# Input projection of a decoder layer: RMS factor applied to the products in place of the input, weights second in the load queue, squares added on VectorE

## The reference, cut to what matters

```python
def rms_norm(x, g):
    xf = x.astype(jnp.float32)
    xf = xf * lax.rsqrt(jnp.mean(xf * xf, axis=-1, keepdims=True) + EPS)
    return xf.astype(x.dtype) * g

def layer_front(x, norm1_g, w_in, q_norm_g, k_norm_g):
    xn = rms_norm(x, norm1_g)
    proj = xn @ w_in
    q, k, v, a, gt = jnp.split(proj, ...)
    q = rms_norm(q.reshape(hs), q_norm_g)     # per head of 64
    k = rms_norm(k.reshape(hs), k_norm_g)
    v = v.reshape(hs)
    u = a * jax.nn.sigmoid(gt)
    return q, k, v, u
```

## Time and profile before

| | us |
|---|---|
| three runs | 1910.13, 1910.41, 1918.43 |
| median | 1910.41 |
| the profiled execution | 1909.07 |
| its span, first to last instruction | 1907.4 |
| TensorE busy in the span | 1809.6 (95%) |
| DVE busy | 1482.6 (78%) |
| POOL busy | 1065.8 (56%) |
| ACT busy | 824.4 (43%) |

### The profile page before, as it was taken

How to read it: one execution, slowest core, us unless ns; L and a number is a source line. 1 busy time by engine, 2 the same in 40 slices (tenths; PEclk the granted TensorE clock), 3 DMA queues, 4 the chain that set the end, 5 groups by cost and what they waited for, 6 DMA issues and landing times.

```text
span 1907.4 us, 38904 instructions
## 1 busy us (share of the span) xinstructions
PE 1809.6 (95%) x14571; PEld 1717.1 (90%) x14571; DVE 1482.6 (78%) x2730; ACT 824.4 (43%) x1101; POOL 1065.8 (56%) x813
## 2 busy tenths in 40 slices
PE   6988988989899999999999999999999999999996
PEld 6988765449899999999999999999999999999995
DVE  3659675541588988985776699999999999999973
ACT  4233665432322445555776444444444444434421
POOL 3232222222224888875564777777777777777720
PEclk8999999989899999999999999999999999999997
DMA  4362877872122677766676999999999999999961
GB/s 158 94 118 99 280 260 271 301 267 97 67 89 96 210 230 229 221 221 207 231 279 263 323 348 349 365 351 360 348 373 354 358 350 375 351 357 358 344 221 69
DMA packets 207319, 488.43 MB, mean 256 GB/s; under 512 B 34161, under 2 KB 119218, under 8 KB 187090
## 3 DMA queue, kind: packets, MB, share of 16 engines
q1 hardware_dynamic: 145474, 315.97, 48.2%
q0 software_dynamic: 55296, 167.94, 23.7%
q10 hardware_dynamic: 6416, 2.78, 1.2%
HBM read 445.95 MB, written 40.66 MB: 255 GB/s over the span
## 4 chain that ended last, share of the span: by engine, by line
PE 84%; DVE 7%; ACT 4%; issue 1%; POOL 1%; DVEq 1%; DMA 1%; ACTq 0%; POOLq 0%
PE pair L1554 24%; PE pair L1556 24%; PE pair L1555 24%; PE pair L1886 3%; DVE conv L1088 3%; PE pair L1699 2%; PE pair L1711 1%; PE pair L1837 1%; PE pair L1751 1%; PE pair L1564 1%; PE pair L1664 1%; PE pair L1686 1%; POOL w_lo L645 1%; ACT page_kt L820 1%; ACT w_hi L968 1%
## 5 line engine op out<-in xcount | busy, mean ns | idle before, releaser
L1554 PE MATMUL pair<-x_hi,w_hi 128*128 128x256 f32 (+2 forms) x2064 | 604.0, 293 | 17.7 <-DVE x_lo L1044 13.7
L1555 PE MATMUL pair<-x_lo,w_hi 128*128 128x256 f32 (+2 forms) x2064 | 596.0, 289 | 0.0
L1556 PE MATMUL pair<-x_hi,w_lo 128*128 128x256 f32 (+2 forms) x2064 | 594.8, 288 | 0.0
L1554 PEld LDWEIGHTS pair<-x_hi,w_hi 128*128 128x128 f32 x2064 | 393.2, 190 | 20.6 <-issue 14.9
L1555 PEld LDWEIGHTS pair<-x_lo,w_hi 128*128 128x128 f32 x2064 | 392.9, 190 | 0.2
L1556 PEld LDWEIGHTS pair<-x_hi,w_lo 128*128 128x128 f32 x2064 | 391.4, 190 | 0.0
L657 POOL DMA_INDIRECT v_rows<-in_v_t,at_row x256 | 302.8, 1183 | 135.2 <-DVE pair L1443 81.7
L1443 DVE SCALAR_TENSOR_TENSOR pair<-v_rows,share,pair 128x1024 f32<-128x1024 f32 x254 | 327.4, 1289 | 23.6 <-issue 0.9
L650 POOL DMA_INDIRECT picked_a<-acts_sparse,at_unit x256 | 284.1, 1110 | 92.4 <-issue 77.7
L1554 PE MATMUL pair<-a_hi,w_hi 128*128 128x288 f32 x1024 | 308.2, 301 | 17.8 <-DVE w_lo L1505 17.8
L1556 PE MATMUL pair<-a_hi,w_lo 128*128 128x288 f32 x1024 | 307.3, 300 | 0.0
(11 more groups left out here) (223 smaller groups left out, 3326.6 us busy)
## 6 DMA issues: line engine op xcount, KB each, us to landing
w_raw<-in_u_t SPq DMA_DIRECT2D x72, 1024.0 KB, 5.2
v_raw<-in_u_t SPq DMA_DIRECT2D x53, 1024.0 KB
w_raw<-in_v_t SPq DMA_DIRECT2D x128, 256.0 KB
v_raw<-in_v_t SPq DMA_DIRECT2D x128, 256.0 KB, 4.4
gates<-g_out SPq DMA_DIRECT2D x9, 2048.0 KB, 8.2
g_in<-gates SPq DMA_DIRECT2D x16, 1152.0 KB
v_ring<-in_cache_v SPq DMA_DIRECT2D x64, 256.0 KB, 3.8
v_ring<-in_cache_v POOLq DMA_DIRECT2D x64, 256.0 KB, 4.4
```

Source lines behind the costliest of these rows:

```text
L1554: te.matmul(out, s_hi, m_hi, start=start, stop=False)
L1555: te.matmul(out, s_hi, m_lo, start=False, stop=False)
L1556: return te.matmul(out, s_lo, m_hi, start=False, stop=stop)
```

## The change

The gain `g1` alone is multiplied into `x` before the split; the token's factor is left out of the projection's input and applied to what comes out of it:

- gates: DVE multiplies the PSUM result by `rstd` into `sq` (`scale_gate`), ACT takes the sigmoid in place, DVE multiplies the sigmoid by `rstd` once more, so that `u = a * (sigmoid * rstd)`;
- q and k: TensorE transposes `rstd` so that the factor stands along the partitions (`turn_rho`, kept by DVE in `rho`); ACT's square takes it as its scale, and DVE's scaling becomes a product with two factors;
- v: ACT's copy takes it as its scale.

The sum of squares: ACT squares the 8 blocks of `x` into the 4 blocks of `q_t` and the 4 of `k_t` (free at that time), DVE adds them in three steps, and TensorE sums over the features once (`sum_first`, a pair of matmuls) inside chunk 1, into `pair[3]`. The order of loads becomes `g1`, `x` part 0, weights 0, `x` parts 1 to 3, weights 1. The low part of chunk 0 moves from POOL to DVE, in two halves. POOL sets `eps` first, and ACT takes a square of it before anything else. Two of the first seven taps move behind the scaling of the second pair of gates.

```diff
+            sp.dma_start(g1[:, :], io["norm1_g"]).then_inc(gain_loaded, 16)
             for part in range(4):
                 two_blocks = slice(2 * part, 2 * part + 2)
                 sp.dma_start(resid[:, two_blocks, :], io["x_t"][:, two_blocks, :]).then_inc(x_loaded[part], 16)
-            load_weights(0)
+                if part == 0:
+                    load_weights(0)
             load_weights(1)
-            sp.dma_start(g1[:, :], io["norm1_g"]).then_inc(small_loaded, 16)
...
-            for chunk in range(N_IN + 1):
+            pool.wait_ge(w_split, 1)
+            for chunk in range(1, N_IN + 1):
...
-            sc.wait_ge(const_ready, 1)
-            squares(sq, resid, KD, lambda kd: sc.wait_ge(x_loaded[kd // 2], 16), sum1_done, sq1_done,
-                    lambda kd: high_w(0) if kd == KD - 3 else None)
-            root(pair[0], D, sum1_done, KD, root1_done)
-            high_x(scaled1, high1)
-            high_w(1)
+            sc.wait_ge(eps_ready, 1)
+            sc.activation(rstd[:, 0:1], eps[:, :], ACT.Square)
+            for kd in range(KD):
+                sc.wait_ge(scaled1, kd + 1)
+                sc.activation(x_hi[:, kd, :], conv[:, kd % 4, :], ACT.Copy).then_inc(high1, 1)
+                if kd == 1:
+                    high_w(0)
+                elif kd == KD - 3:
+                    high_w(1)
+                sc.activation(squared(kd), resid[:, kd, :], ACT.Square).then_inc(sq1_done, 1)
+            high_w(2)
+            root(pair[3], D, sum1_done, 1, root1_done)
...
                 for cb in range(2):
-                    sc.wait_ge(projected, 2 * chunk + cb + 1)
-                    if n:
-                        sc.wait_ge(u_done, cb + 1)
-                    sc.activation(two(sq[:, cb, :]), halves(pair[cb]), ACT.Sigmoid).then_inc(gate_sig, 1)
-                high_w(chunk + 2)
+                    sc.wait_ge(gate_scaled, 2 * n + cb + 1)
+                    sc.activation(sq[:, cb, :], sq[:, cb, :], ACT.Sigmoid).then_inc(gate_sig, 1)
+                if n:
+                    high_w(chunk + 2)
...
+            def scale_x(kd):
+                v.wait_ge(x_loaded[kd // 2], 16)
+                v.tensor_scalar(conv[:, kd % 4, :], resid[:, kd, :], g1[:, kd:kd + 1], None, ALU.mult).then_inc(scaled1, 1)
+            def low_x(kd):
+                v.wait_ge(high1, kd + 1)
+                v.tensor_tensor(x_lo[:, kd, :], conv[:, kd % 4, :], x_hi[:, kd, :].bitcast(F32), ALU.subtract)\
+                    .then_inc(x_ready, 1)
+            def low_first_w():
+                v.wait_ge(w_high, 1)
+                for first in (0, WC // 2):
+                    mine = slice(first, first + WC // 2)
+                    last = v.tensor_tensor(w_lo[:, 0, mine], w_raw[:, 0, mine], w_hi[:, 0, mine].bitcast(F32), ALU.subtract)
+                last.then_inc(w_split, 1)
+            v.wait_ge(gain_loaded, 16)
+            scale_x(0)
+            for kd in range(1, KD):
+                scale_x(kd)
+                low_x(kd - 1)
+                if kd == 2:
+                    low_first_w()
+            low_x(KD - 1)
+            v.wait_ge(sq1_done, KD)
+            v.tensor_tensor(q_t[:, :, :], q_t[:, :, :], k_t[:, :, :], ALU.add)
+            v.tensor_tensor(q_t[:, 0:2, :], q_t[:, 0:2, :], q_t[:, 2:4, :], ALU.add)
+            v.tensor_tensor(q_t[:, 0, :], q_t[:, 0, :], q_t[:, 1, :], ALU.add).then_inc(squares_added, 1)
...
-            normed(g1, root1_done, scaled1, high1, x_ready)
+            reciprocal_rms(root1_done)
+            def scale_gate(n):
+                for cb in range(2):
+                    v.wait_ge(projected, after_projection(2 * n) - 1 + cb)
+                    v.tensor_tensor(two(sq[:, cb, :]), halves(pair[cb]), two(rstd[:, :]), ALU.mult).then_inc(gate_scaled, 1)
...
             for n in range(2):
+                scale_gate(n)
+                if n:
+                    taps_of(0, 2)
+                for cb in range(2):
+                    v.wait_ge(gate_sig, 2 * n + cb + 1)
+                    v.tensor_tensor(sq[:, cb, :], sq[:, cb, :], rstd[:, :], ALU.mult)
...
                 if n == 0:
-                    taps_of(0, FIRST_TAPS)
+                    taps_of(0, FIRST_TAPS - 2)
+            v.wait_ge(rho_turned, 1)
+            v.tensor_copy(rho[:, 0:NT - 1], pair[1][:, 1, 0:P].rearrange("p (t x) -> p t x", x=32)[:, :, 0])
+            v.tensor_copy(rho[0:NDEC, NT - 1:NT], pair[1][0:NDEC, 1, P:P + 1]).then_inc(rho_kept, 1)
...
-                    v.tensor_tensor(dst.rearrange("p (h d) -> p h d", d=HD),
-                                    pair[m % 4 // 2][0:r, m % 2, 0:WCOL].rearrange("p (h d) -> p h d", d=HD),
-                                    ss.unsqueeze(2).to_broadcast([r, 4, HD]), ALU.mult).then_inc(qk_scaled, 1)
+                    v.scalar_tensor_tensor(dst.rearrange("p (h d) -> p h d", d=HD),
+                                           pair[m % 4 // 2][0:r, m % 2, 0:WCOL].rearrange("p (h d) -> p h d", d=HD),
+                                           rho[0:r, nt:nt + 1], ss.unsqueeze(2).to_broadcast([r, 4, HD]),
+                                           ALU.mult, ALU.mult).then_inc(qk_scaled, 1)
...
-            te.wait_ge(const_ready, 1)
-            sum_squares(pair[0], sq, KD, sq1_done, sum1_done)
+            def sum_first():
+                te.wait_ge(squares_added, 1)
+                te.wait_ge(const_ready, 1)
+                for half in range(2):
+                    last = te.matmul(pair[3][:, half, 0:HALF], ones[:, :], q_t[:, 0, HALF * half:HALF * (half + 1)],
+                                     start=True, stop=True)
+                last.then_inc(sum1_done, 1)
+            def turn_rho():
+                for nt in range(NT):
+                    r = ROWS[nt]
+                    last = te.transpose(pair[1][0:r, 1, 32 * nt:32 * nt + 32], rstd[0:32, P * nt:P * nt + r], ident[0:32, 0:32])
+                last.then_inc(rho_turned, 1)
...
-                    te.wait_ge(root1_done, 1)
                     chunk_product(0, x_ready)
...
-                    if chunk == 2:
-                        te.wait_ge(gate_sig, cb + 1)
+                    if chunk == 1 and cb == 1:
+                        te.wait_ge(root1_done, 1)
+                    elif chunk == 2:
+                        te.wait_ge(gate_scaled, cb + 1)
...
-                    block_product(banks, chunk % 2, cb).then_inc(projected, 1)
+                    between = (lambda n: sum_first() if n == 1 else None) if chunk == 1 and cb == 0 else None
+                    block_product(banks, chunk % 2, cb, between).then_inc(projected, 1)
...
                     if m == 0:
-                        te.wait_ge(gate_sig, 4)
+                        te.wait_ge(gate_scaled, 4)
+                        turn_rho()
+                    elif m == 3:
+                        te.wait_ge(rho_kept, 1)
```

More of the change, by code:

```diff
@@ L382, in build_layer, with squared @@
     up_done, gelu_done, a_done, down_done, added = sem("up_done"), sem("gelu_done"), sem("a_done"), sem("down_done"), sem("added")
-    SMALL_LOADS = 7
+    eps_ready, gain_loaded, squares_added = sem("eps_ready"), sem("gain_loaded"), sem("squares_added")
+    gate_scaled, rho_turned, rho_kept = sem("gate_scaled"), sem("rho_turned"), sem("rho_kept")
+    rho = stats[:, 80:80 + NT]
+    def squared(kd):
+        return (q_t if kd < PAIRS else k_t)[:, kd % PAIRS, :]
+    SMALL_LOADS = 6
     STORES = 4 + 2 + 1 + CC
@@ L597, in _ @@
         def _(pool):
+            pool.memset(eps[:, :], EPS).then_inc(eps_ready, 1)
             pool.memset(ones[:, :], 1.0)
@@ L601, in _ @@
             pool.memset(own[:, :, :], 0.0)
-            pool.memset(eps[:, :], EPS)
             pool.memset(u_p[:, :, 0:PAD], 0.0)
@@ L760, in _ @@
                             sc.wait_ge(u_done, 4)
-                        sc.activation(sq[0:r, m % 2, 0:WCOL], src, ACT.Square).then_inc(qk_sq, 1)
+                        sc.wait_ge(rho_kept, 1)
+                        sc.activation(sq[0:r, m % 2, 0:WCOL], src, ACT.Square, scale=rho[0:r, nt:nt + 1]).then_inc(qk_sq, 1)
                         sc.wait_ge(qk_sum, m + 1)
@@ L766, in _ @@
                     else:
-                        sc.activation(v_nat[0:r, nt, WCOL * (chunk - 4):WCOL * (chunk - 3)], src, ACT.Copy)\
+                        sc.activation(v_nat[0:r, nt, WCOL * (chunk - 4):WCOL * (chunk - 3)], src, ACT.Copy, scale=rho[0:r, nt:nt + 1])\
                             .then_inc(v_kept, 1)
@@ L1054, in normed @@
                 low(KD - 1)
+            def scale_x(kd):
[5 more added lines that the diff above has]
+                    .then_inc(x_ready, 1)
+                if kd % 2:
+                    v.drain()
+            def low_first_w():
[14 more added lines that the diff above has]
+            v.tensor_tensor(q_t[:, :, :], q_t[:, :, :], k_t[:, :, :], ALU.add)
+            v.drain()
+            v.tensor_tensor(q_t[:, 0:2, :], q_t[:, 0:2, :], q_t[:, 2:4, :], ALU.add)
+            v.drain()
```

(2 more changed lines are left out.)

## The result

The kernel after the change takes 1957.91 us (median; 1953.46 to 1962.09), the kernel before beside it 1910.78 (1910.13 to 1918.43). The ratio is 1.0235, interval 1.0211 to 1.0259: **2.4% slower**, 47 us, where 1899.9 was forecast. The profiled execution of after took 1953.46, its span is 1951.8.

What follows compares the result with a forecast made beforehand. TensorE was taken as the bound (84% of the chain), behind a front delay of 24.58 us. Terms -11.8 - 0.2 - 0.6 + 1.05 + 0.75 + 0.3 = -10.5 took 1910.41 to 1899.9 us, range 1897.5 to 1904.5.

Steps and rivals of the forecast that it cites:

- Start: Front of the kernel: TensorE's first product comes at 12.75 us in place of 24.58, worth -11.8 us.
- Clock: TensorE's first products: low clock for 2.9 to 5.9 us (13 to 26 products), taken as -0.6 us.
- Summing pair: TensorE's queue in chunk 1: one added pair of matmuls summing the squares, +1.05 us.
- Transposes: TensorE's queue: five added transposes of rstd, about +0.75 us, range 0.4 to 1.2.
- The covers: Projection chunks: new waits for squares, root, reciprocal, gates and chunk 4's weights hidden by slack, the last 1.6 to 2.3 us.
- Rival A: Chunk 4's weights: thin cover gives way, TensorE 2.5 to 3 us late, total 1903; chance 0.20.
- rival B: DVE is the bound: its added 5.1 us find no idle time, gain 5.4, total 1905; chance 0.10.
- The collision: Chunk 1: low_x(6) on DVE waits for POOL's low part until 22.7 us, costing TensorE 0 to 0.3 us.
- Products with two factors: DVE's 20 tiles: 0.782 against 0.721 us each, +0 to +1.2 us, taken +0.3.
- the whole shifts: Everything after the front (attention, output projection, mixer) moves earlier by the front's whole gain, -10.5 us.
- Rival D: TensorE's clock stays low beyond chunk 0; 1916.5 us if chunks 0 and 1 are all low; chance 0.03.
- C: Start doesn't matter, a later stage being set by something that doesn't move (pages, stores); about 1909 us; chance 0.05.

Runs made afterwards that it cites:

- e1: Changed kernel with 46 instructions of fulfilled waits ahead of TensorE's first product; 1980.1 against 1995.82 us for the kernel before, ratio 0.9935.
- e5: Changed kernel with 46 instructions of waiting ahead of TensorE's work, timed in more rounds; 1982.29 against 1997.2 us for the kernel before, ratio 0.9927.
- e6: Changed kernel with 46 waiting instructions, low part of weights 0 back on POOL in one piece; 1987.9 us, ratio 0.9954 to the kernel before.
- e7: Changed kernel with 46 waiting instructions, weights 0 loaded behind all four parts of x again; 1982.36 us, ratio 0.9949 to the kernel before.
- e8: Kernel before with only weights 0 issued between the first and second part of x; 1996.34 us, ratio 1.0005 to the kernel before.
- e10: Changed kernel with 37 instructions of waiting ahead of TensorE's work; 1977.2 us in one run, kernel before beside it 1983.18.
- e11: Changed kernel with 225 instructions of waiting ahead of TensorE's work; 2010.41 us in one run.
- e4: Changed kernel with 24 instructions of fulfilled waits ahead of TensorE's first product; 2046.75 us, ratio 1.0287 to the kernel before.
- e9: Changed kernel with 33 instructions of waiting ahead of TensorE's work; 2061.2 us in one run, kernel before beside it 1983.18.
- e2: Kernel before with 210 instructions of fulfilled waits in TensorE's queue behind the sums of the squares; 2039.99 us, ratio 1.0258 to the kernel before.
- e12: Changed kernel with 250 instructions of waiting ahead of TensorE's work; 2038.64 us in one run.

## Why the prediction was wrong, point by point

- **Start** (-11.8): measured 12.69 against the worked-out 12.75, **-11.9**. Right, with each term of its queue: scale 2 at 9.05, the low part of weights 0 at 10.28, two halves in 2.36.
- **Clock** (-0.6): low for 3.9 us, inside the 2.9 to 5.9 that were given; 17 products in place of 26, -0.9.
- **Summing pair** (+1.05): 29.61 to 30.33, **+0.72**, cheaper than half of the row of eight passes (2.10): in that row, at the granted clock 1.00, the first pass after 1.16 us of idleness holds up the second for 0.34, and the last counts with its whole 0.39, while in after passes start 0.23 apart and the next product 0.03 behind the last one. **Transposes** (+0.75): 63.91 to 64.30, about **+0.4**.
- **The covers.** No wait at the pair, at `pair[3]`, at the gates or at chunk 4; TensorE waits for nothing from 12.69 to 64.30. But the slack of chunk 4 was thinner than said. POOL's low part ended at 63.35 and was wanted at 64.30: 0.95 us, not 1.6 to 2.3. Rival A came near.
- **DVE** (rival B): its 17 us of waiting were used up wholly. It was busy 35.62 of the 36.80 us from 27.5 to 64.3. Yet TensorE never waited for it there. Some 13 us of this are three instructions that stretched to 4.59, 4.71 and 4.65 us beside POOL's low parts; plain they take 0.24 to 0.54. The first of them, at 28.89, put the reciprocal off to 33.77, though the root was there at 31.45, and its end to 37.31, where the prediction has 36.0.
- **The collision** of the earlier trace rows came as forecast: POOL's low part of chunk 1 ran from 17.98 to 22.62, and two blocks of `low_x` took 4.89 us beside it (0.72 for one elsewhere) without making TensorE wait. The sigmoids' product ran at 38.91 and 64.15, beside no low part of POOL's, so what the prediction says of its stall was not put to the test.
- **Products with two factors** (+0.3): of 11.7 us at the first q tile 10.7 are left at 187, so some +1.0 in the stage of the tiles, inside the +0 to +1.2 given, though the runs didn't separate this term from others of that stage.
- **The step that failed** is the last one: "Everything after the front ... waits for semaphores of the layer itself, ... so the whole shifts." The times did shift; the program shifted as well. The sum listed what each removed instruction costs in its place and took its going for pure gain: "The squares' 32 passes lay ahead of the product and their going is in the start already." That they also stood ahead of a loop in TensorE's code had no term. Its price, 56.8 us, is five times the gain. Rival D named a loss on TensorE, but by the clock in the front, and that rival did not occur; C put its doubt in loads of data, and its "all loads wait for semaphores" overlooked the instruction queue, which stood on the page of before with 79 packets.
- What stays unshown: that the changed kernel with its code put back takes about 1900 on the chip of the forecast. On two others it gained 13.0 and 14.6 us; the forecast's 10.5 is in both intervals. That version is ahead of the kernel before on both chips.

## What to carry to other kernels

A change of the instruction count ahead of a long loop can be a change of the loop, as it was for TensorE here. Before trusting a sum, count the body's instructions in blocks of the instruction queue's packets; if it is close to what the engine keeps, compare that queue's packets before and after, and look for "issue" waits at regular distances. When a front is right to a tenth of a microsecond and the total is not, look for the place where the two traces drift apart, and there for waits with no releaser.

## What the runs showed of the hardware

**A loop refetches all or nothing, by the place of its code.** The same loop, some 1,585 instructions, ran without any fetch stop where it touches seven blocks of 256 (before, e1, e5 to e8, e10, e11: 79 or 80 packets), and stopped TensorE where it touches eight: at all six jumps in after, e4 and e9 (133 packets), at four of six in e2 and e12 (116). What decides between six and four isn't shown. A jump fetches nine packets or none. The window of shifts that run well has one edge between 33 and 37 instructions and the other between 225 and 250. With 16 products between the two fetches a jump cost 4.1 to 5.9 plus 1.1 to 2.2 us of stops (after, e2), with four 4.1 to 5.4 plus 4.1 to 5.0 (e4), with none 9.5 to 10.9 (e9). That the count of blocks is what matters is shown by both edges. That it comes from a buffer of eight blocks, in which the fetch of a ninth, begun when the eighth is entered, overwrites the first, is only argued; it would also make the case of e2 and e12 a race, in which a jump taken soon enough finds the first block still there, and time, not place, would then decide. No run separates this from other accounts.

The Trainium skill ("Runtime: NRT & Kernel Launch", section "Instruction fetch mechanics") states the blocks of 256 instructions in 16 KiB, a buffer of 2,048 instructions for TensorE, and that a taken branch to a target outside the current two pages has to fetch it. The packets agree with the blocks (2.18 MB in 133). The rule of two pages doesn't hold here: by it the kernel before would stop at each jump too, as its loop is over six blocks long, and its TensorE has no such wait. The measurement decides.

**Idle code isn't free.** 420 and 450 fulfilled waits (210 and 225 instructions) put the first product off by 15.3 and 17.5 us where they lay on its path (39.92 against 24.58 and 30.51 against 13.02), while with 92 of them (46 instructions) the first product, at 12.96 and 13.22, still waits for DVE's low part of the weights and not for them.
